# A cached decoder step on one core: when and in what pieces the window caches are copied

## The reference, cut to what matters

```
for buf, kn, vn in zip(bufs, split_groups(k_new), split_groups(v_new)):
    kk = concatenate([buf[:, :, 0], kn], axis=1)
    vv = concatenate([buf[:, :, 1], vn], axis=1)
    new_bufs.append(stack([kk[:, t_new:], vv[:, t_new:]], axis=2))     # t_new = 4
```

## Time and profile before

| | us |
|---|---|
| time, median of 3 runs | 688.44 |
| the three runs | 687.83, 688.44, 694.17 |
| profiled execution, from its first to its last instruction (span) | 683.4 |
| TensorE busy in that span | 614.2 (90%) |
| DMA packets over the span, of 16 engines' time: SyncE's queue, GpSimd's queue | 41.6%, 39.7% |

### The profile page before, as it was taken

How to read it: one execution, slowest core, us unless ns; L and a number is a source line. 1 busy time by engine, 2 the same in 40 slices (tenths; PEclk the granted TensorE clock), 3 DMA queues, 4 the chain that set the end, 5 groups by cost and what they waited for, 6 DMA issues and landing times.

```text
span 683.4 us, 13785 instructions
## 1 busy us (share of the span) xinstructions
PE 614.2 (90%) x4870; PEld 428.3 (63%) x4870; DVE 377.5 (55%) x1150; ACT 167.9 (25%) x405; POOL 224.5 (33%) x406
## 2 busy tenths in 40 slices
PE   6899999898989978979999999988899997898994
PEld 3676565565667755647777665566656775565772
DVE  3754655777759535433147475577766953543213
ACT  3015322121113202550111352312211320235111
POOL 2207540242106675451000475123120667541000
PEclk9999999998889998999999999999989999799897
DMA  8939999999978899995333799999998889993111
GB/s 333 374 133 315 367 369 408 418 346 356 350 246 270 308 315 371 351 293 204 113 115 141 263 369 369 395 408 376 367 361 297 276 307 310 371 332 121 54 69 69
DMA packets 67766, 198.38 MB, mean 290 GB/s; under 512 B 11537, under 2 KB 40370, under 8 KB 66418
## 3 DMA queue, kind: packets, MB, share of 16 engines
q1 hardware_dynamic: 49682, 99.99, 41.6%
q0 software_dynamic: 18016, 97.50, 39.7%
HBM read 189.30 MB, written 52.00 MB: 353 GB/s over the span
## 4 chain that ended last, share of the span: by engine, by line
PE 57%; DMA 18%; DVE 14%; SPq 4%; ACT 4%; issue 3%; DVEq 0%; ACTq 0%
PE bank L825 55%; DMA w<-in_w 6%; DMA kv<-in_kk 6%; DMA kv<-in_vv 5%; SPq L404 3%; DVE hit L1452 3%; PE bank L875 2%; DVE tb L1465 1%; DVE st L1954 1%; DMA ptab<-in_ptab 1%; ACT srow L766 1%; ACT shared L663 1%; DVE shared L1575 1%; ACT shared L680 1%; DVE tb L1463 1%
## 5 line engine op out<-in xcount | busy, mean ns | idle before, releaser
L825 PE MATMUL bank<-xn,w 128*128 128x288 f32 x1120 | 304.2, 426 | 4.7 <-DMA w<-in_w 4.7
L825 PEld LDWEIGHTS bank<-xn,w 128*128 128x128 f32 x1120 | 212.3, 197 | 78.4 <-issue 17.4
L404 POOL DMA_DIRECT2D kv<-in_kk x128 | 68.8, 538 | 153.6 <-issue 98.1
L404 POOL DMA_DIRECT2D kv<-in_vv x160 | 86.4, 540 | 99.3 <-PE bank L825 72.7
L616 ACT ACTIVATE pt<-bank 128x288 f32<-128x288 f32 x48 | 19.6, 409 | 237.7 <-PE bank L825 237.7
L825 PE MATMUL bank<-pt,w 128*128 128x288 f32 x256 | 65.2, 410 | 0.0
L825 PEld LDWEIGHTS bank<-pt,w 128*128 128x128 f32 x256 | 48.8, 192 | 14.1 <-issue 0.7
L496 POOL DMA_DIRECT2D out_keep<-in_buf x48 | 23.5, 495 | 81.3 <-PE bank L825 73.3
L825 PE MATMUL bank<-kv,pt 128*32 128x256 f32 x512 | 38.2, 406 | 11.5 <-DMA kv<-in_vv 11.3
L1452 DVE TENSOR_SCALAR_CACHE_REDUCE hit<-sc,tb 128x516 bf16<-128x516 f32 x62 | 46.5, 750 | 2.2
L2022 DVE TENSOR_TENSOR x<-x,bank 128x288 f32<-128x288 f32 x16 | 7.3, 454 | 50.2 <-PE bank L825 50.1
(11 more groups left out here) (238 smaller groups left out, 802.8 us busy)
## 6 DMA issues: line engine op xcount, KB each, us to landing
w<-in_w SPq DMA_DIRECT2D x86, 512.0 KB, 7.6
out_keep<-in_buf POOLq DMA_DIRECT2D x16, 2044.0 KB, 14.3
kv<-in_kk SPq DMA_DIRECT2D x128, 160.0 KB, 8.8
kv<-in_kk POOLq DMA_DIRECT2D x128, 160.0 KB, 5.8
kv<-in_vv POOLq DMA_DIRECT2D x160, 128.0 KB, 5.3
kv<-in_dil SPq DMA_DIRECT2D x24, 576.0 KB, 8.2
kv<-in_vv SPq DMA_DIRECT2D x96, 128.0 KB, 5.1
out_keep<-in_buf POOLq DMA_DIRECT2D x16, 508.0 KB, 8.8
```

What stands on the lines that cost most here:

```text
L404: engine.dma_start(kv[:, s, r * rec:(r + 1) * rec], a["kk" if what == "page" else "vv"][bass.ds(page + layer * N_POOL, 1)].rearrange("o p ...
L825: return pe.matmul(out, lhsT, rhs, start=start, stop=stop, skip_group_check=True, **k)
```

## The change

Three things change. A copy is now issued with `max_dma_last_dim=4096`, which caps one descriptor (one contiguous piece that a DMA engine moves) at 4,096 bytes. `keep` takes the layer as an argument. And the places differ: sequence 0 is copied behind the fifth tile, `proj4`, ahead of the page stage; sequences 1 to 4 in the search stage behind `proj16`, `proj18`, `proj20` and `proj22`; sequences 5, 6 and 7 of the first layer behind `out0`, `out2` and `out4`, with sequence 6 of the second layer behind the first layer's `out6`; sequences 5 and 7 of the second layer behind its `proj34` and `out0`. The bytes copied are the same.

```
-                def keep(b, use):
+                def keep(of, b, use):
                     pool.wait_ge(filled(use), nth(L, use))
                     for g in range(3):
-                        pool.dma_start(a[f"keep{g}"][ly, b], a[f"buf{g}"][ly, b, 4 * 256:]).then_inc(S["copied"], 16)
+                        pool.dma_start(a[f"keep{g}"][bass.ds(of, 1), b], a[f"buf{g}"][bass.ds(of, 1), b, 4 * 256:],
+                                       max_dma_last_dim=4096).then_inc(S["copied"], 16)
...
+                keep(L, 0, "proj4")
                 for u in range(NPAIR):
...
-                keep(0, "proj16")
+                keep(L, 1, "proj16")
                 pool.wait_ge(S["roped"], nth(L, "roped", 9))
                 feat(KI, KI + 1, 0, "ki_out")
                 feat(KA, KA + 2, 1)
-                keep(1, "proj17")
-                keep(2, "proj18")
+                keep(L, 2, "proj18")
                 pool.wait_ge(S["xws_ready"], nth(L, "xws_ready", 1))
                 masked(0)
                 masked(1)
-                keep(3, "proj19")
-                keep(4, "proj20")
-                keep(5, "proj21")
+                keep(L, 3, "proj20")
...
-                keep(6, "proj23")
-                keep(7, "proj24")
+                keep(L, 4, "proj22")
                 consumed(*RING[32:40])
...
                 consumed(*RING[66:])
+                if L + 1 < DEPTH:
+                    for b, use in ((5, "out0"), (6, "out2"), (7, "out4")):
+                        keep(L, b, use)
+                    keep(L + 1, 6, "out6")
+                else:
+                    keep(L, 5, "proj34")
+                    keep(L, 7, "out0")
                 for name in ("ki_out", "feat_out", "tail_out", "h_out"):
                     pool.wait_ge(S[name], nth(L, name, PER[name]))
```

## The result

The changed kernel takes **733.7 us** (median of 4 runs, 732.8 to 734.59) against 691.11 us for the kernel before beside it: a ratio of 1.0614, 95% interval 1.0551 to 1.0676. It is 6% slower; I had forecast 685.4 us, in a range of 682 to 692. The profiled execution took 734.17 us with a span of 732.5, so only 1.7 us lie around the span; the 5.0 us that I had put there were mostly the scatter of runs. Every ratio here compares only runs within 1.5% of the fastest of their kernel; the profiled executions of `e3_no_copies`, `e4_places_whole_lines` and `e6_places_19k` lie beyond that, so their spans are no measure of those kernels.

The account below looks back on a forecast made before the run. Search stage bound by a VectorE-TensorE loop, DMA mattering only where a weight tile is late; page stage by DMA. Only -3.06 us counted, other terms nothing: 688.44 - 3.06 = 685.4 us, range 682 to 692.

Parts of the forecast that it names:

- What a copy costs the DMA engines: All copies: one sequence's copy takes 7.6 us of all 16 engines, also in small pieces; at most 11.4 us.
- the bound of 11.4: Upper limit in us for one copy, half as much again for writing HBM in small pieces; kernel then 701.7 us.
- capped that at 2.7 us: Behind the first layer's outputs: a late weight tile costs nothing, at most 2.7 us once.
- Smaller descriptors: a gain where weights were late: Search stage: smaller pieces let weights land within 7.9 us, so the wait ahead of `proj26` goes, -3.06 us.
- The 3.06 us: First layer's search stage: 1.30 us wait for a weight plus slower matmuls behind it, all to be gained.
- no effect: Late weight tile comes from one slow DMA engine, or ordinary runs have no wait there: 688.4 us, chance 0.12.
- The places: Four copies behind the outputs and a fifth behind second-layer `proj4` fit narrowly, at no cost; room 8.1 us each.
- The search stage's share: DMA share in the search stage, with four copies instead of eight, falls from 0.99 to about 0.6.
- GpSimd's queue: Issuing a copy takes at most 2.2 us instead of 0.495, and nothing waits for it: no cost.
- The two last copies: Second layer's end, started at about 624 and 645: each done within some 15 us, inside the span, no cost.
- spill: Copies before the second page stage not done at 380, delaying page loads: 688 to 702 us, chance 0.15.

Follow-up runs that it names:

- e3_no_copies: The kernel before with the three copies in `keep` deleted, so shifted caches are not returned: 688.32 us, ratio 0.9982.
- e4_places_whole_lines: The changed kernel with caps that cut the three windows into pieces of 3,968, 8,128 and 4,672 bytes, all multiples of 64: 687.83 us, ratio 0.9985.
- e6_places_19k: The changed kernel with caps of 7,936, 32,512 and 18,688 bytes, all whole lines: 701.6 us, ratio 1.0116.
- e5_whole_lines_only: The kernel before, copies at their old places, with pieces of 3,968, 8,128 and 4,672 bytes: 688.65 us, ratio 0.9998.
- e1_places_only: The changed kernel without the cap, so new places with pieces of up to 65,408 bytes: 702.28 us, ratio 1.0211.
- e8_one_window: The changed kernel with one number changed, a cap of 4,672 for the 2044 KB window: 687.63 us, ratio 0.9975.

## Why the prediction was wrong

**The step that failed** is the term "What a copy costs the DMA engines". I took 7.6 us because queues of small and of large packets cost the same 2.8 us for each MB; it is 11.2 us, near the bound of 11.4 that I had drawn and then given little weight. The small packets that I went by were loads into SBUF: 4,096 bytes for weights, 4,096 and 5,120 in GpSimd's queue. None is a write to HBM in pieces off a line, and the length of the piece, 2,093,056 / 512 = 4,088, could have been worked out from the diff and was not. With whole lines the number was right: in `e4_places_whole_lines` the copies' packets take 120.9 us of 16 engines, 7.6 for each copy, the share behind the outputs is 0.94, five copies fit, and the time is 687.83 us.

**The bound was priced wrongly too.** At 11.4 us for a copy I had reckoned 701.7 us, by engine time left over at the page loads. That mechanism is there (6.2 us in the second page stage, and 11.2 in the first, where I had the copy done at 53 us in the worst case and it landed at about 63). But the larger part, 13.4 + 12.5 us, came by late weights, 18.8 us of it as waits and most of the rest as slower tiles behind them: I had capped that at 2.7 us, once, since I took slow copies as slow for themselves. They slowed the weights beside them: SyncE's queue took 34.3 us more for the same bytes, and behind the outputs weights landed after 24.7 us in the median and 35.0 at most, where I had estimated 7.9 at most.

**"Smaller descriptors: a gain where weights were late": right in its mechanism, nil in its worth.** With whole lines in the old places (`e5_whole_lines_only`) the landings fall from 18.1 and 34.0 us to 8.5 and 10.0, close to the estimate, and there is no wait for a weight in the search stage. The time does not follow: 0.9998. The 3.06 us were one wait in one execution, while runs of the kernel before reach from 683 to 699 us; even without any copy the ratio is 0.9982. The rival "no effect" was right for the kernel that I thought I was judging.

**The places: right.** The free time behind the outputs takes four copies and the front a fifth, but narrowly; that small pieces are needed there is shown by `e1_places_only`, 2% slower (1.2 to 3.0). The search stage's share falls to 0.61 from 120 to 210 in `e8_one_window`, where I had put 0.6; the changed kernel's own share stayed at 0.98.

**GpSimd's queue: right.** The issue of a copy takes 0.563 us on average instead of 0.495, and nobody waits for it. The two last copies end inside the span in every version: the stretch behind `out7` is 11.6 us before and after.

**Chances.** The true case, spill with late weights, had 0.15 with "spill" and its own arithmetic ended at 702. The base of the range, that each rival's price is what its own mechanism costs, left out that a slow writer takes everyone's bandwidth.

## What to carry to other kernels

Before capping or splitting a DMA to HBM, work out the length of the piece: it is the row divided by a count, not the cap, and 4,088 where 4,096 was meant made this copy 1.8 times as long by itself and 6% of the kernel's time. Choose a length that is a multiple of 64 bytes (32 was enough here), if need be a bigger one, such as 4,672. Where a new kind of transfer has no row in the trace, rows of another direction or alignment are no estimate of it; and when an engine shared by all gets slower, price the neighbours' loads too.

## What the runs showed of the hardware

- HBM to HBM, four copies of about 2 MB, written one behind another with nothing else running: pieces of 4,088 bytes take 52.2 us for what takes 28.9 in pieces of 4,032 and 28.7 in 4,064; from SyncE's queue it is 51.3, so it is not GpSimd's way of making descriptors.
- Pieces of about 4 KB written 8 bytes off a line take 33.0 us one behind another and 29.9 with gaps between them, where a start on the line takes 29.9 too.
- The order is not one of fineness alone: 4,080 takes 32.4, 4,092 takes 36.1, and 4,096 with both ends 56 bytes off 33.5. Why 4,088 stands out among them stays open; no run tells it.
- The copy's slowness is shared: at a DMA share of 1.01, 226 GB/s moved behind the outputs, against 354 at a share of 0.94 in the same stretch with whole lines (`e4_places_whole_lines`).
